# A hybrid decoder step on one core: where VectorE's evictions of the attention levels stand in the second mixer

## Chip, core and metric

The kernel runs on one NeuronCore of a Trainium2 chip. The metric is the device time of one launch in microseconds (us), the median of several runs. Engines are called TensorE (PE in the rows, PEld for its weight loads), VectorE (DVE), ScalarE (ACT), GpSimd (POOL) and SyncE (SP, which issues the DMAs). Each runs its own instructions strictly in their order and waits on semaphores.

## What is computed

Two decoder layers run over 512 new prompt tokens and 32 sample tokens (8 sequences of 4): a half-step SwiGLU feed-forward, a token mixer, a second feed-forward and a gated per-layer embedding. The first layer's mixer is GLA, the second's is HGRN2. Both rest on one recurrence with a decay per channel; within a block of tokens it is exact pairwise attention:

```python
def chunked_gated_linear_recurrence(q, k, v, g, s0, scale):
    # S_t = diag(exp(g_t)) S_{t-1} + k_t^T v_t ; o_t = scale * q_t S_t
    ...
        b = jnp.cumsum(gc, axis=1)
        rel = b[:, :, None] - b[:, None, :]
        decay = jnp.exp(jnp.where(mask, rel, -jnp.inf))
        attn = jnp.einsum('bthk,bshk,btshk->bhts', qc, kc, decay) * scale
        o_intra = jnp.einsum('bhts,bshv->bthv', attn, vc)
        o_inter = jnp.einsum('bthk,bhkv->bthv', qc * jnp.exp(b), S) * scale
        k_dec = kc * jnp.exp(b_last[:, None] - b)
        S_new = S * jnp.exp(b_last)[..., None] + jnp.einsum('bshk,bshv->bhkv', k_dec, vc)

def hgrn2_mixer(u, w_in, gn, w_out, lb, s0):
    q, f, i, g = jnp.split(u @ w_in, cuts, axis=-1)
    log_f = jnp.logaddexp(jnp.log(lb), jnp.log1p(-lb) + jax.nn.log_sigmoid(f))
    k = (1.0 - lb) * jax.nn.sigmoid(-f)
    o, s = chunked_gated_linear_recurrence(heads(jax.nn.silu(q)), heads(k), heads(i), heads(log_f), s0, 1.0)
    o = rms_norm(o, gn) * jax.nn.silu(heads(g))
    return o.reshape(B, T, HGRN_I_DIM) @ w_out, s
```

## The kernel before

Every matmul with weights is done three times, on a high and a low part of both operands, to keep float32 accuracy. Weights come in units of 512 KB through a ring of four slots; ScalarE copies the high part (`high`), VectorE subtracts it for the low part (`low`, the tile `w_low`). `ahead(n)` does this two units ahead of TensorE.

Each mixer is done in two head groups, numbered 0 and 1 (GLA, 2 heads each) and 2 and 3 (HGRN2, 4 heads each). The attention of a 128-token chunk is split by levels. Level l takes blocks of 2L tokens (L = 2 to the l, l from 0 to 6) and computes the second half's queries against the first half's keys; the decay across the half's border is put into the two factors. For each level:

- VectorE sums the gates up to the block (`level_gates`, L2043, tile `gate_sum`) and takes the differences to the border (`level_diffs`, L2031, tile `ex`), both in place for the level to come.
- ScalarE takes their exponentials (`level_keys` L1424 for the differences, `level_queries` L1408 for the sums).
- VectorE multiplies keys and queries with them (`level_keys` L2059, tile `k_tilde`; `level_queries` L2087, tile `q_tilde`). In the GLA groups GpSimd does the queries' part.
- TensorE computes eight blocks of 128 x 128 (L828) into PSUM banks 4 and 5 (banks 6 and 7 for level 5).
- VectorE (ScalarE for levels 5 and 6) copies the wanted parts under a mask into the tile `attn` (`level_out`, the *eviction*, L2010; for levels 0 and 1 also a small one for the sample tokens, L1999 and L2019).

In groups 2 and 3 levels 0 to 4 share banks 4 and 5, so TensorE's level l waits for the eviction of level l - 1 (semaphore `lvl_out`) besides the products of its own level (`kt_made`, `qt_made`). Between the levels TensorE computes other tiles of the same stage, by a table written out by hand (`gr.steps`): gate tile g0, four units of the value matmul (L773) with levels 0 to 3 behind them, gate tile g1 with levels 4 and 5 behind it, g2 with level 6, and at last g3. The value matmul fills banks 0 to 3 and 7. Gate tile g1 uses banks 0 and 1 and waits until ScalarE has evicted the first two value tiles (`values_out`, L1386, semaphore `v_out`); on ScalarE these evictions stand behind the two exponentials of level 4, the other three behind those of level 5.

Behind the levels (`mix`), VectorE evicts g2 (L1881), makes the keys' decays to the chunk's end (L2152, L2156), splits two weight units (L1677) and multiplies the decays into the keys (L2165, semaphore `kdec_made`). TensorE transposes these keys (L863) after g3. SyncE loads the sample states in two halves of four DMAs (L477): the first when all levels are computed, the second when the decays of all keys are in, since the destination overlaps tiles that are read until then. TensorE's products with those states (L902) wait for all of them (`s0_in`).

Of the kernel before, what the change touches and what calls it, by code (L numbers as in the profile page):

```python
# [154 lines left out]
def _build(nc, a, o, ctx):  # L155
# [128 lines left out]
    def halves(ap):  # L284
        return ap.rearrange("p (a b) -> p a b", a=2)
# [57 lines left out]
    def samples(t, gr):  # L343

        return t[:, gr.NH * T_PROMPT:gr.NH * T]
# [1326 lines left out]
    def _(dve):  # L1672
# [235 lines left out]
        def features(gr):  # L1908
            n = gr.start
            qs = [(Q, h, gr.q_scale if gr.gla else None) for h in range(gr.NH)]  # L1910
            ks = [(K, h, None) for h in range(gr.NH)]
            dests = ([(RT, None, None)] if gr.has_r else []) + (qs + ks if gr.gla else ks + qs)
            if gr.gi == 1:

                dve.wait_ge(s["x_out"], 4)
                dve.tensor_copy(halves(G[:, 0:2 * T_PROMPT]), OG[:, 6:8, 0:T_PROMPT])
                dve.tensor_copy(halves(samples(G, gr)), OG[:, 6:8, T_PROMPT:T]).then_inc(s["x_made"], 1)
                dve.wait_ge(s["x_made"], 1)
            for j, (dst, h, scale) in enumerate(dests):
                if not gr.gla and j == 5:  # L1920
                    log_sigmoid(gr)
                    gate(gr)
                    head_out(gr, j, n, dst, h, scale)
                    gate_diff(gr)
                    ahead(n)
                    gate_key(gr)
                    n += 1
                    continue
                if not gr.gla and j == 7:
                    gate_end(gr)  # L1930
                ahead(n)
                if gr.gi == 1 and j == 1:
                    log_sigmoid(gr)
                if gr.g == 1 and j == 0:
                    dve.wait_ge(s["og_made"], 2 * gr.gi)
                    dve.wait_ge(s["og_made_p"], 2 * gr.gi)
                if h is None:
                    feature_out(gr, j, n, dst)
                else:
                    head_out(gr, j, n, dst, h, scale)  # L1940
                n += 1
                if gr.g == 0 and j == 1:
                    sample_tokens(gr)
                if gr.g == 1 and j in (0, 2):
                    sequences(GROUPS[gr.gi - 1], j // 2)
                if gr.has_r and j >= gr.nfeat - 2:
                    gates_out(gr, range(2) if j == gr.nfeat - 2 else (2,))
            if gr.gi == 0:
                log_sigmoid(gr)
            for kind, j, levels in gr.steps[:-2]:  # L1950
                ahead(n)
                n += 1
                for lv in levels:
                    if lv == "diag":
                        if gr.gla:
                            level_gates(gr, 0)
                        feature_out(gr, gr.nfeat, n - 1, OG[:, 4 * gr.g, :])
                        if not gr.gla:
                            level_queries(gr, 0)
                            level_gates(gr, 0)  # L1960
                        if gr.has_r:
                            gates_out(gr, (3,))
                        diagonal(gr)
                        level_diffs(gr, 1)
                    elif lv and lv < 4:
                        level(gr, lv)
                        level_out(gr, lv - 1)
            level(gr, 4)
            level_out(gr, 3)
            level(gr, 5)  # L1970
            ahead(n)
            feature_out(gr, gr.nfeat + 1, n, OG[:, 4 * gr.g + 1, :])
            level_out(gr, 4)
            level_keys(gr, 6)
            if not gr.gla:
                level_queries(gr, 6)
            level_gates(gr, 6)
            if gr.gla:
                ahead(n + 1)
            else:  # L1980
                feature_out(gr, gr.nfeat + 2, gr.g3_unit - 1, OG[:, 4 * gr.g + 2, :])
# [9 lines left out]
        def level_out(gr, l):  # L1991
            gi, NH = gr.gi, gr.NH
            n, L = LEVELS * gi + l, 1 << l
            b0 = gr.level_bank(l)
            dve.wait_ge(s["lvl_mm"], n + 1)

            if l == 0:
                S = T_SAMPLE
                dve.tensor_tensor(ATS[0:S, 0:NH, :], ps[0:S, 6, 0:NH * 32].rearrange("p (x n) -> p x n", x=NH),  # L1999
                                  ident[0:S, 0:S].rearrange("p (o n) -> p o n", o=1).to_broadcast([S, NH, S]),  # L2000
                                  ALU.mult).then_inc(s["sdiag_out"], 1)
                dve.wait_ge(s["diag_out"], gi + 1)
                dve.wait_ge(s["sdiag_out"], gi + 1)
            else:
                dve.wait_ge(s["lvl_out"], n)
            if l == 1:
                dve.wait_ge(s["slvl_out"], 2 * gi + 1)
            msk = [(0, 2 * NH), (L, 64 // L), (1, L)]
            for r in range(2):
                ins = dve.copy_predicated(query_half(AT, gr, L, r), view(masks[:, l, r, :].bitcast(U32), 0, msk),  # L2010
                                          compact(psf[:, 512 * b0:512 * b0 + 1024], gr, L, r))
            ins.then_inc(s["lvl_out"], 1)
            if l < 2:
                S = T_SAMPLE
                dst = ATS[0:S, 0:NH, :].rearrange("p x (n l) -> p x n l", l=2 * L)[:, :, :, L:2 * L]
                data = ps[0:S, 6, (8 + 4 * l) * 16:(8 + 4 * l + NH) * 16].rearrange("p (x n l) -> p x n l", x=NH, l=L)
                msk = masks[0:S, l, 0, 0:S // 2].bitcast(U32).rearrange("p (o n l) -> p o n l", o=1, l=L)\
                    .to_broadcast([S, NH, 16 // L, L])
                dve.copy_predicated(dst, msk, data).then_inc(s["slvl_out"], 1)  # L2019

        def level_diffs(gr, l):

            gi, L = gr.gi, 1 << l
            dve.wait_ge(s["gate_made"], (LEVELS + 1) * gi + l + 1)
            if l > 1:
                dve.wait_ge(s["kt_made"], (LEVELS - 1) * gi + l - 1)
            if l == 1:
                g1, _, tot = sample_blocks(G, gr, L)
                dve.tensor_tensor(sample_compact(DK, gr, L), tot, g1, ALU.subtract)
            for r in range(2):  # L2030
                ins = dve.tensor_tensor(compact(DK, gr, L, r), last_key(G, gr, L, r), key_half(G, gr, L, r), ALU.subtract)  # L2031
            ins.then_inc(s["diff_made"], 1)

        def level_gates(gr, l):

            n, L = LEVELS * gr.gi + l, 1 << l
            dve.wait_ge(s["eq_made"], n + 1)
            if l < 2:
                _, g2, tot = sample_blocks(G, gr, L)
                dve.tensor_tensor(g2, g2, tot, ALU.add)  # L2040
            for r in range(2):
                g2 = query_half(G, gr, L, r)
                ins = dve.tensor_tensor(g2, g2, last_key(G, gr, L, r), ALU.add)  # L2043
            ins.then_inc(s["gate_made"], 1)
# [15 lines left out]
                                        compact(DK, gr, L, r), ALU.mult)  # L2060
            ins.then_inc(s["kt_made"], 1)

        def level(gr, l):

            level_keys(gr, l)
            if not gr.gla:
                level_queries(gr, l)
            level_gates(gr, l)
            level_diffs(gr, l + 1)

        def level_queries(gr, l):

            gi, L = gr.gi, 1 << l
            n = LEVELS * gi + l
            dve.wait_ge(s["eq_made"], n + 1)
            if l >= 2:
                dve.wait_ge(s["lvl_mm"], n - 1)
            if l == 0:
                if gr.g == 1:
                    dve.wait_ge(s["lvl_mm"], LEVELS * gi)  # L2080
                dve.wait_ge(s["feat_out"], gr.feat0 + gr.nfeat)
                dve.wait_ge(s["q_made"], 2 * (gi - 1))
            if l < 2:
                dve.tensor_tensor(QTS[:, l, 0:gr.NH * 16].rearrange("p (n l) -> p n l", l=L),
                                  sample_blocks(Q, gr, L)[1], sample_compact(EQ, gr, L), ALU.mult)
            for r in range(2):
                ins = dve.tensor_tensor(compact(QTb[:, l % 2, :], gr, L, r), query_half(Q, gr, L, r),  # L2087
                                        compact(EQ, gr, L, r), ALU.mult)
            ins.then_inc(s["qt_made"], 1)
# [417 lines left out]
```

## Time and profile before

| | |
|---|---|
| median of 3 runs | 2235.97 us (2233.2 to 2236.51) |
| the profiled execution | 2235.69 us, its span 2233.3 us |
| TensorE busy | 2213.9 us (99%), granted clock 0.997 on the mean |
| VectorE busy | 1577.2 us (71%) |
| ScalarE busy | 1083.9 us (49%) |
| GpSimd busy | 332.3 us (15%) |

The two head groups of the second mixer compute their levels from about 1517 to 1568 us and from about 1657 to 1708 us. In the rows a time at the head of a line is microseconds from the span's start, the next number how long the instructions of the line took together. An instruction gives way to the next on its engine a little ahead of its end, so a line may overlap the next. A bracket names the idle time of the engine just before and what ended it.

### The profile page before, as it was taken

What the parts mean: (1) busy time and instruction counts of PE and PEld (TensorE: products, weight loads), DVE (VectorE), ACT (ScalarE), POOL (GpSimd) and SP (SyncE); (2) the same over time, 40 slices, a digit from 0 to 9 for tenths busy, and PEclk for the clock granted to TensorE, in tenths of its full rate; (3) what the DMA queues carried; (4) which work ended last, traced back from release to release, by engine and by line L of the source; (5) the groups of instructions that cost most, each with busy time, mean ns of one, the idle gap of its engine ahead of it and who ended that gap; (6) DMA issues with size and microseconds to landing.
All of it is one profiled execution on the core that took longest, in us unless ns stands there. A gap on an engine that the chain in (4) does not pass through costs nothing. (4 is left out here: it accounts for less than half of the span.)

```text
span 2233.3 us, 42317 instructions
## 1 busy us (share of the span) xinstructions
PE 2213.9 (99%) x17778; PEld 2168.5 (97%) x17778; DVE 1577.2 (71%) x2172; ACT 1083.9 (49%) x1573; POOL 332.3 (15%) x239
## 2 busy tenths in 40 slices
PE   9999999999999999999999999999999999999998
PEld 8999999989999999999999999998999999999998
DVE  7888833567678888535788884359688788886344
ACT  7555622443555555423655562255465565555234
POOL 3222101112111221000222210000000212220001
PEclk9999999999999999999999999999999999999999
DMA  4333333233352333333233333322333333333231
GB/s 136 102 107 95 102 100 83 58 105 93 102 137 76 107 102 102 91 102 86 67 110 99 95 100 95 105 71 67 91 95 105 104 91 95 111 97 107 83 96 49
DMA packets 387338, 213.36 MB, mean 96 GB/s; under 512 B 7007, under 2 KB 381438, under 8 KB 387150
## 3 DMA queue, kind: packets, MB, share of 16 engines
q1 hardware_dynamic: 386928, 210.59, 33.6%
q8 instruction: 140, 2.29, 0.4%
q14 instruction: 48, 0.39, 0.1%
q10 hardware_dynamic: 190, 0.05, 0.0%
q0 software_dynamic: 32, 0.03, 0.0%
HBM read 198.98 MB, written 11.67 MB: 94 GB/s over the span
## 5 line engine op out<-in xcount | busy, mean ns | idle before, releaser
L642 PE MATMUL ps<-u_diffs,w_high 128*128 128x272 f32 x2560 | 486.8, 288 | 2.3 <-DVE w_low L1773 1.7
L642 PEld LDWEIGHTS ps<-u_diffs,w_high 128*128 128x128 f32 x2560 | 402.1, 188 | 3.2 <-issue 3.0
L642 PE MATMUL ps<-u_diffs,w_low 128*128 128x272 f32 x1280 | 369.3, 289 | 0.0
L1677 DVE TENSOR_TENSOR w_low<-w_raw,w_high 128x1024 fp32r<-128x1024 f32 x205 | 259.1, 1281 | 98.1 <-ACT w_high L1136 97.8
L2399 POOL TENSOR_TENSOR hidden<-t_gate,t_up 128x544 f32<-128x544 f32 x84 | 190.1, 2263 | 717.7 <-ACT t_gate L1258 717.7
L570 PE MATMUL ps<-hid_high,w_high 128*128 128x272 f32 x1408 | 290.4, 287 | 0.0
L570 PE MATMUL ps<-hid_high,w_low 128*128 128x272 f32 x1408 | 289.5, 288 | 0.0
L570 PE MATMUL ps<-hid_low,w_high 128*128 128x272 f32 x1408 | 289.1, 287 | 0.0
L642 PE MATMUL ps<-u_high,w_low 128*128 128x272 f32 x960 | 277.5, 289 | 0.0
L642 PE MATMUL ps<-u_low,w_high 128*128 128x272 f32 x960 | 276.9, 288 | 0.0
L642 PE MATMUL ps<-u_high,w_high 128*128 128x272 f32 x960 | 275.9, 287 | 0.3 <-DVE w_low L1773 0.3
L1136 ACT ACTIVATE w_high<-w_raw 128x1024 fp32r<-128x1024 f32 x205 | 210.4, 1049 | 113.4 <-PE ps L570 73.6
L570 PE MATMUL ps<-u_high,w_high 128*128 128x272 f32 (+2 forms) x1168 | 245.7, 292 | 2.2 <-DVE u_low L1690 1.8
L642 PEld LDWEIGHTS ps<-u_diffs,w_low 128*128 128x128 f32 x1280 | 240.6, 188 | 0.0
L570 PE MATMUL ps<-u_high,w_low 128*128 128x272 f32 (+2 forms) x1168 | 240.4, 288 | 0.0
L570 PE MATMUL ps<-u_low,w_high 128*128 128x272 f32 (+2 forms) x1168 | 240.3, 287 | 0.0
L1773 DVE TENSOR_TENSOR w_low<-w_sums,w_high 128x512 fp32r<-128x512 f32 (+1 forms) x240 | 208.6, 869 | 21.5 <-ACT w_high L1227 20.5
L570 PEld LDWEIGHTS ps<-hid_low,w_high 128*128 128x128 f32 x1408 | 220.1, 188 | 0.0
L570 PEld LDWEIGHTS ps<-hid_high,w_low 128*128 128x128 f32 x1408 | 219.3, 188 | 0.0
L570 PEld LDWEIGHTS ps<-hid_high,w_high 128*128 128x128 f32 x1408 | 219.2, 188 | 0.0
L1161 ACT ACTIVATE u_high<-h_resid,vectors 128x544 fp32r<-128x544 f32 x48 | 36.1, 751 | 372.7 <-DVE h_resid L1873 322.3
L570 PEld LDWEIGHTS ps<-u_high,w_high 128*128 128x128 f32 x1168 | 184.1, 188 | 5.6 <-DVE u_low L1690 2.4
(292 smaller groups left out, 4093.7 us busy)
## 6 DMA issues: line engine op xcount, KB each, us to landing
w_raw<-in_ffn_w_gu_dram SPq DMA_DIRECT2D x176, 512.0 KB, 5.2
w_raw<-in_ffn_w_down_dram SPq DMA_DIRECT2D x64, 512.0 KB, 4.5
w_raw<-in_hgrn_w_in_dram SPq DMA_DIRECT2D x32, 512.0 KB, 4.7
w_raw<-in_gla_w_in_dram SPq DMA_DIRECT2D x25, 512.0 KB, 5.0
w_raw<-in_ffn_w_down_dram SPq DMA_DIRECT2D x32, 384.0 KB, 4.5
w_raw<-in_ple_w_gate_dram SPq DMA_DIRECT2D x16, 512.0 KB, 4.9
states_s<-in_state_gla_dram SPq DMA_DIRECT2D x8, 512.0 KB, 5.9
out_gla_s_dram<-states_s SPq DMA_DIRECT2D x8, 512.0 KB, 3.8
```

The costliest lines, as they stand in the source:

```text
L570: mm = pe.matmul(ps[:, bank + hf, 0:t1 - t0], weights(slot, w0 + k, wk, m0, P, kw), x[:, kk - w0, t0:t1], start=(kk == 0 and part == 0), s ...
L642: mm = pe.matmul(ps[:, bank, 0:HALF], half_slot(w, base, h)[:, k * P:(k + 1) * P], x(k), start=start and k == 0 and part == 0, stop=k == K ...
L1136: act.activation(WH[:, slot, :], RAW[:, slot, :], ACT.Copy).then_inc(s["hi_made"], 1)
L1161: act.activation(flat_of(UH, m), flat_of(H, m), ACT.Copy, scale=gain_of(e, m)).then_inc(s["uh_done"], 1)
L1677: dve.tensor_tensor(WL[:, slot, :], RAW[:, slot, :], WH[:, slot, :].bitcast(F32), ALU.subtract)\
L1773: dve.tensor_tensor(half_slot(WL, base, h, n), src, half_slot(WH, base, h, n).bitcast(F32), ALU.subtract)\
L2399: pool.tensor_tensor(HID[:, f, :], tG[:, :], tU[:, :], ALU.mult).then_inc(s["hid_mul"], 1)
```

## The change

In the HGRN2 groups, the eviction of level l - 1 moves, for l from 1 to 4, from behind the gate sums of level l and the differences of level l + 1 to a place ahead of them, right behind the products of level l. The eviction of level 4 stays where it was, and so does everything in the GLA groups. TensorE's, ScalarE's, GpSimd's and SyncE's instructions and their order are the same.

```diff
@@ features
                     elif lv and lv < 4:
                         level(gr, lv)
-                        level_out(gr, lv - 1)
             level(gr, 4)
-            level_out(gr, 3)
-            level(gr, 5)
+            level(gr, 5, False)
@@ level
-        def level(gr, l):
+        def level(gr, l, out=True):
 
             level_keys(gr, l)
             if not gr.gla:
                 level_queries(gr, l)
+                if out:
+                    level_out(gr, l - 1)
             level_gates(gr, l)
             level_diffs(gr, l + 1)
+            if gr.gla and out:
+                level_out(gr, l - 1)
```

VectorE in group 2, level 1 and the start of level 2, before (`w_low` is a weight split, `ex` the differences, `attn` and `attn_s` the evictions):

```order
L2087 TENSOR_TENSOR q_tilde<-q,ex 128x8x64 x2
L2040 TENSOR_TENSOR gate_sum<-gate_sum 128x32x2
L2043 TENSOR_TENSOR gate_sum<-gate_sum 128x8x32x2 x2
L2031 TENSOR_TENSOR ex<-gate_sum 128x8x64 x2
L1999 TENSOR_TENSOR attn_s<-ps,ident 32x128
L2010 COPY_PREDICATED attn<-masks,ps 128x8x64 x2
L2019 COPY_PREDICATED attn_s<-masks,ps 32x64
L1677 TENSOR_TENSOR w_low<-w_raw,w_high 128x1024
L2059 TENSOR_TENSOR k_tilde<-k,ex 128x128x4 x2
```

The same place on VectorE after the change (the lines from L1964 on are two lower):

```order
L2089 TENSOR_TENSOR q_tilde<-q,ex 128x8x64 x2
L1997 TENSOR_TENSOR attn_s<-ps,ident 32x128
L2008 COPY_PREDICATED attn<-masks,ps 128x8x64 x2
L2017 COPY_PREDICATED attn_s<-masks,ps 32x64
L2038 TENSOR_TENSOR gate_sum<-gate_sum 128x32x2
L2041 TENSOR_TENSOR gate_sum<-gate_sum 128x8x32x2 x2
L2029 TENSOR_TENSOR ex<-gate_sum 128x8x64 x2
L1677 TENSOR_TENSOR w_low<-w_raw,w_high 128x1024
L2057 TENSOR_TENSOR k_tilde<-k,ex 128x128x4 x2
```

The three instructions of the eviction of level 0 have moved up past the three of the sums and differences; the weight split still stands between the differences and the key products.

VectorE in group 2, level 4 and the start of level 5, before:

```order
L2059 TENSOR_TENSOR k_tilde<-k,ex 128x32x16 x2
L2087 TENSOR_TENSOR q_tilde<-q,ex 128x8x64 x2
L2043 TENSOR_TENSOR gate_sum<-gate_sum 128x8x4x16 x2
L2031 TENSOR_TENSOR ex<-gate_sum 128x8x64 x2
L2010 COPY_PREDICATED attn<-masks,ps 128x8x8x8 x2
L2059 TENSOR_TENSOR k_tilde<-k,ex 128x16x32 x2
L2087 TENSOR_TENSOR q_tilde<-q,ex 128x8x64 x2
```

The same place on VectorE after the change:

```order
L2057 TENSOR_TENSOR k_tilde<-k,ex 128x32x16 x2
L2089 TENSOR_TENSOR q_tilde<-q,ex 128x8x64 x2
L2008 COPY_PREDICATED attn<-masks,ps 128x8x8x8 x2
L2041 TENSOR_TENSOR gate_sum<-gate_sum 128x8x4x16 x2
L2029 TENSOR_TENSOR ex<-gate_sum 128x8x64 x2
L2057 TENSOR_TENSOR k_tilde<-k,ex 128x16x32 x2
L2089 TENSOR_TENSOR q_tilde<-q,ex 128x8x64 x2
```

The eviction of level 3 has moved up past the sums and differences, and the key products of level 5 now follow the differences directly. The same holds one level earlier.

## Rows read from the trace of the kernel before

**Rows 1.** The page's first part: busy time of TensorE, share, instructions.

```profile
PE 2213.9 (99%) x17778; PEld 2168.5 (97%) x17778; DVE 1577.2 (71%) x2172; ACT 1083.9 (49%) x1573; POOL 332.3 (15%) x239
```

**Rows 2.** TensorE's waits over the span: us in total, times, longest.

```profile
PE ps L828 <- DVE attn L2010: 2.8, 4, 1.0
PE ps L1094 <- ACT y_feat L1147: 2.6, 1, 2.6
```

**Rows 3.** Timeline of TensorE: last value matmul, levels 1, 2; level 1 again, group 3.

```profile
1530.43 0.40 PE L773 MATMUL ps<-w_low,u_high 128*128 128x512 f32 x1
1531.84 0.57 PE L828 MATMUL ps<-q_tilde,k_tilde 128*128 128x128 f32 x3 [1.01 <-DVE attn L2010]
...
1540.36 0.91 PE L828 MATMUL ps<-q_tilde,k_tilde 128*128 128x128 f32 x6 [0.40 <-DVE attn L2010]
...
1671.49 0.68 PE L828 MATMUL ps<-q_tilde,k_tilde 128*128 128x128 f32 x4 [1.02 <-DVE attn L2010]
```

**Rows 4.** Timeline of VectorE, group 2, sums of level 1 to eviction of level 0.

```profile
1526.17 0.21 DVE L2040 TENSOR_TENSOR gate_sum<-gate_sum 128x64 f32<-128x64 f32 x1
...
1527.63 1.29 DVE L2031 TENSOR_TENSOR ex<-gate_sum 128x512 f32<-128x512 f32 x2
1528.84 0.27 DVE L1999 TENSOR_TENSOR attn_s<-ps,ident 32x128 f32<-32x128 f32 x1
1529.21 2.48 DVE L2010 COPY_PREDICATED attn<-masks,ps 128x512 f32<-128x512 uint32 x2
```

**Rows 5.** Timeline of VectorE, group 2, differences of level 4 on; query products of level 5.

```profile
1545.03 1.30 DVE L2031 TENSOR_TENSOR ex<-gate_sum 128x512 f32<-128x512 f32 x2
1546.24 1.33 DVE L2010 COPY_PREDICATED attn<-masks,ps 128x512 f32<-128x512 uint32 x2
1547.55 1.29 DVE L2059 TENSOR_TENSOR k_tilde<-k,ex 128x512 f32<-128x512 f32 x2
...
1555.02 1.28 DVE L2087 TENSOR_TENSOR q_tilde<-q,ex 128x512 f32<-128x512 f32 x2
```

**Rows 6.** Timeline of ScalarE, group 2, exponentials of level 4 and first value tiles.

```profile
1546.36 1.06 ACT L1424 ACTIVATE ex<-ex 128x1024 f32<-128x1024 f32 x1 [6.43 <-DVE ex L2031]
1547.33 1.14 ACT L1408 ACTIVATE ex<-gate_sum 128x512 f32<-128x512 f32 x2
1549.18 1.27 ACT L1386 ACTIVATE v_tok<-ps,rstd_tok 128x512 f32<-128x512 f32 x2 [0.72 <-PE ps L773]
```

**Rows 7.** Timeline of TensorE, group 2, level 3 and the start of level 4.

```profile
1548.98 1.95 PE L828 MATMUL ps<-q_tilde,k_tilde 128*128 128x128 f32 x16
...
1556.75 0.72 PE L828 MATMUL ps<-q_tilde,k_tilde 128*128 128x128 f32 x5
```

**Rows 8.** Timeline of VectorE, group 2, eviction of gate tile g2 and key decays.

```profile
1566.51 0.72 DVE L1881 TENSOR_TENSOR out_gate<-ps,rstd 128x544 f32<-128x544 f32 x1 [1.06 <-PE ps L570]
...
1571.83 2.49 DVE L2165 TENSOR_TENSOR k<-k,ex 128x1024 f32<-128x1024 f32 x2
```

**Rows 9.** Timeline of SP's queue, the last state load of groups 2 and 3.

```profile
1576.54 0.51 SPq L477 DMA_DIRECT2D states_s<-in_state_hgrn_dram  x1
...
1715.50 0.51 SPq L477 DMA_DIRECT2D states_s<-in_state_hgrn_dram  x1
```

**Rows 10.** DMA issues, these two loads: count, KB each, us to landing.

```profile
states_s<-in_state_hgrn_dram SPq DMA_DIRECT2D x1, 256.0 KB, 5.0
...
states_s<-in_state_hgrn_dram SPq DMA_DIRECT2D x1, 256.0 KB, 5.1
```

**Rows 11.** Timeline of TensorE, products with the sample states, groups 2 and 3.

```profile
1581.62 0.65 PE L902 MATMUL ps<-states_s,q 128*32 128x128 f32 x16 [0.27 <-issue]
...
1720.92 0.84 PE L902 MATMUL ps<-states_s,q 128*32 128x128 f32 x21
```

**Rows 12.** Stretches near the end: busy PE, PEld, DVE, ACT, POOL; granted clock; DMA.

```profile
2218.00:2220.00 2.00, 0.46 (x5) 0.22 (x2) 1.45 (x4) 0.83 (x2) 0.00 (x0) 1.00 0.00 0
...
2224.00:2226.00 2.00, 1.79 (x9) 1.69 (x10) 1.48 (x2) 1.57 (x5) 0.00 (x0) 0.50 0.00 0
```

## Prediction, on record before the run

> **What bounds the kernel now.** I read the engines' shares first, then who TensorE waited for, then the timelines of TensorE, VectorE and ScalarE through the second mixer, then the DMA queue. TensorE is busy 2213.9 of 2233.3 us [rows 1]: a change can only take away what little it idles, or add idle time. Its largest wait in total is for the block evictions on VectorE, four times, 2.8 us [rows 2]. All four lie in the second mixer: before levels 1 and 2, in head group 2 (near 1531 and 1540 us) and again in head group 3 (near 1671 and 1680) [rows 3]. The view counts from a matmul's modelled end. Counted from the step of the value matmuls (0.23 us, from one start to the next), TensorE could have gone on at 1530.43 + 0.23 = 1530.66 and went on at 1531.84: 1.18 us lost. The view gives 1.01 of that; its 0.40 at level 2 is 0.56 counted so. The first matmuls after each wait cost some 0.07 more. **So the stalls that the change aims at are worth 1.25 + 0.63 = 1.9 us per head group, 3.8 us in all, 0.17% of the run.** A measurement of this kernel can tell about 0.2% (4.5 us) from no change; even the whole gain is below that. Group 3 runs the same pattern 139.65 us later, so I work out group 2 and carry it over.
>
> **Part 1, the evictions come earlier (gain 1.9 us per group at first).** VectorE's slot after the query products of level 1 opens at 1526.17. Before, it holds the gate sums; the differences follow at 1527.63, the eviction of level 0 at 1529.21, 2.48 long, and TensorE starts 0.15 after its end [rows 3, 4]. After, the sample eviction takes this slot (it takes 0.37 up to the main one, by 1528.84 and 1529.21), the main one runs from 1526.54 to 1529.02, and TensorE, free at 1530.66, does not wait. The same holds at level 2: TensorE gets there 1540.36 - 0.56 - 1.25 = 1538.55; the eviction of level 1, which ended 0.15 ahead of 1540.36, moves up by the 2.53 of a level's sums and differences (from 1526.17 to 1528.84, less 0.14 for the small sum at its head) less the 0.14 of part 2, and ends at 1537.8. Level 3 had no wait and has none.
>
> **Part 2, what the eviction had covered is open now (VectorE 2.74 us late).** From the differences' start of level l+1, ScalarE's exponential starts 1.33 us later (1545.03 to 1546.36), and the key products that need it 1.19 after that (1546.36 to 1547.55): 2.52 in all. The differences fill 1.21 of it, up to 1546.24 [rows 5, 6]. Before, the eviction of the level below stood in the other 1.31, up to 1547.55. Its own share is some 1.23 (it lasts 1.33, less the 0.1 by which such instructions overlap: the differences last 1.30 and give way after 1.21); 0.08 was waiting even then. After, it takes its 1.23 ahead of the sums, and where nothing else stands in the gap, the 1.31 pass empty: 1.23 lost. At levels 2 and 3 a weight split of some 1.18 us still stands there (1.23 long), so only about 0.14 is lost each time. At levels 4 and 5 nothing does. VectorE's lateness against the old times: 0.14 at level 2's keys, 0.28 at level 3's, 1.51 at level 4's, 2.74 at level 5's (2 x 0.14 + 2 x 1.23). The gap ahead of level 6 is covered by a weight split, the gate eviction and the eviction of level 4, in both kernels, and stays at 2.74.
>
> **Part 3, where TensorE meets this (the 1.9 us are gone at the next gate tile).** Behind level 3 TensorE computes gate tile g1 in PSUM banks 0 and 1. It must wait until ScalarE has evicted the first two value tiles from them, and ScalarE does that only behind the two exponentials of level 4. Before: exponentials at 1546.36 and 1547.33, values from 1549.18, 1.27 long, done at 1550.45; TensorE begins g1 at about 1550.9, behind the sixteen matmuls that it starts at 1548.98 (16 in 1.95 us), unhindered [rows 6, 7]. The exponentials hang on the differences of level 4, which are now 1.51 late, so they start at 1547.9 and 1548.9, the values at 1549.9, done at 1551.2, and g1 starts at 1551.3. TensorE would be there at 1550.86 - 1.9 = 1548.96. **It waits about 2.4 us, and g1 begins 0.45 later than before.** After g1, level 4 begins at 1557.2 instead of 1556.75. Level 5 needs the query products that end 2.74 late, at 1559.05: TensorE, there at 1559.15, starts at 1559.25, 0.6 late. Level 6 and the transposes behind it follow 0.8 to 0.9 late by the same addition.
>
> **Part 4, the state loads (what sets the end of each group).** Before, VectorE has 1.06 us of idle time ahead of the eviction of gate tile g2; that takes up part of the 2.74, and TensorE's g2 itself ends about 0.8 late, so the eviction and all behind it are 2.74 - 1.14 = 1.6 late (the idle time plus the 0.08 by which an instruction gives way ahead of its end), the decays of the keys at 1571.83 among them [rows 8]. The second half of the sample-state loads waits in SP's queue for just these decays. Its last load, issued at 1576.54, takes 5.0 us to land: 1581.54 [rows 9, 10]. TensorE starts the products with these states at 1581.62 after 0.27 us of idle time that the view calls issue [rows 11]: 0.08 after the landing, so I take it that this load already ended the wait. With the load 1.6 late, group 2 is 1.6 us late. In group 3 the load lands at 1715.50 + 5.1 = 1720.60 and TensorE comes at 1720.92, 0.24 us of slack after the same 0.08: 1.6 - 0.24 = 1.36, more than the 0.9 by TensorE's own way.
>
> **What lies under cover.** The weight splits late by up to 2.74 are for g3 and for the next stage's units; g3 is needed 5 us or more after its split. The next loads of weights go behind the state loads in SP's queue, for tiles used over 15 us later. GpSimd has no part in these levels. The first mixer keeps its order.
>
> **Sum.** 1.6 + 1.36 is 2.96. The profiled execution took 2235.69 us (2.4 more than its span, unchanged by this) and stands 0.3 below the median of the three runs: 2235.69 + 2.96 = 2238.65, and I predict 2238.7.
>
> **A rule against the trace, twice.** The last state load takes 5.0 and 5.1 us [rows 10]. The Trainium skill, "DMA: Bandwidth & Descriptors" (Anatomy of one DMA, SWDGE path), gives a transfer about 2 us plus its bytes at 436 GB/s; by an estimate from that page 256 KB alone would take 2.6 us, and by it the loads would be hidden. The rows here disagree, for four loads issued 0.5 us apart behind one another. The second rule is at rival 3.
>
> **Rivals.**
> 1. Gain only, 2235.69 - 3.8 = 2231.9: if g1 did not wait for ScalarE (the semaphore of the value tiles is in the code, but the trace of before shows no wait there). Against it: ScalarE's queue order is fixed, and slack was just 0.4 us.
> 2. The loads are hidden and TensorE's own way decides: 0.9 per group, 2237.5. For it: landings can vary, and 0.7 us less would do.
> 3. The clock falls. At the end of the program TensorE waits 2.6 us for ScalarE [rows 2], its busy time falls to 0.46 of 2 us, and the granted clock goes from 1.00 to 0.50, from 2.4 to 1.2 GHz [rows 12], some microseconds later. The new wait before g1 is 2.4 us long. If it does the same, half the rate over g1's 5.9 us costs up to 5.9 per group, over half of it 3: 2238.65 + 6 to 12, taken as 2244.7. It decides only where the clock falls in both or one of the groups. Against it: in the tail few and tiny matmuls followed the wait; here dense ones stand on both sides. The Trainium skill, "TensorE: Matmul & The Clock Gate" (Part 1: The HAM clock gate), says too that an idle array is put back to half rate; the tail agrees, no row shows it for a wait between dense matmuls.
> 4. The loads land later than before (they then share the DMA engines with weight loads at another place): 0.8 us more in each group gives 2240.3, beyond that the run is slower by over 0.2%.
> That the change doesn't do what it says is no rival: the order of VectorE shows it.
>
> **Chances.** Forecast 0.59; rival 1 0.07; rival 2 0.12; rival 3 0.14; rival 4 beyond 0.8 us 0.08. Faster by over 0.2% would need rival 1 and a low run: 0.02. Slower by over 0.2%: rivals 3 and 4 and a little of the noise, 0.22. Within 0.2%: 0.76. The range leaves out rival 1 and the far part of rival 3: from 2235.5 (rival 2 less the 2 us by which runs of one kernel differ) to 2243.5. The forecast's own range is 2237.3 to 2240.
>
> **What would show it.** Right: no wait for the evictions before levels 1 and 2; a wait of about 2.4 us before g1 for ScalarE's value tiles, with the granted clock at 1.00; VectorE idle for some 1.2 us ahead of the key products of levels 4 and 5; the key decays 1.6 us later against the query products of level 1, and a longer wait before the state products. Wrong: g1 without a wait (Part 3), key products of level 5 as early as before (Part 2), the state loads landing well ahead of TensorE (Part 4).

## The result and the profile after

The changed kernel took 2243.11 us (median of 6 runs, 2241.42 to 2243.94), the kernel before 2235.57 us beside it (6 runs, 2232.96 to 2236.51): a ratio of 1.0031, 95% interval 1.0020 to 1.0042. It is 7.5 us slower, by more than the 0.2% that can be told from no change. On another occasion, with 27 runs of the kernel before beside it, it was 2242.09 against 2236.22 (ratio 1.0029, 1.0018 to 1.0040). The forecast was 2238.7; the time lies in the range and near the 2244.7 of rival 3.

The profiled execution after took 2243.67 us, 7.98 more than the one before; its span is 8.5 longer. The first lines of its page, against [rows 1]:

```profile
span 2241.8 us, 42317 instructions
PE 2222.1 (99%) x17778; PEld 2177.3 (97%) x17778; DVE 1577.0 (70%) x2172; ACT 1083.9 (48%) x1573; POOL 333.3 (15%) x239
```

The same instructions are there, and VectorE and ScalarE are as busy as before. TensorE is busy 8.2 us longer with the same 17778 matmuls. So all but 0.3 us of the loss is busy time: **the matmuls themselves ran slower somewhere.** TensorE's waits (us in total, times, longest), against [rows 2]:

```profile
PE ps L570 <- ACT v_tok L1386: 4.6, 2, 2.4
PE ps L1094 <- ACT y_feat L1147: 2.6, 1, 2.6
PE ps L902 <- issue: 0.2, 1, 0.2
```

The four waits for the evictions, 2.8 us, are gone. In their place stand two for the value tiles on ScalarE, ahead of gate tile g1, one in each head group, 4.6 us. The timeline of TensorE through group 2, against [rows 3] and [rows 7] (start, length together, idle time before in the bracket):

```profile
1531.45 0.39 PE L773 MATMUL ps<-w_low,u_high 128*128 128x512 f32 x1
1531.68 0.38 PE L828 MATMUL ps<-q_tilde,k_tilde 128*128 128x128 f32 x2
...
1539.57 0.83 PE L828 MATMUL ps<-q_tilde,k_tilde 128*128 128x128 f32 x6
...
1548.11 1.95 PE L828 MATMUL ps<-q_tilde,k_tilde 128*128 128x128 f32 x16
1552.19 0.82 PE L570 MATMUL ps<-u_high,w_high 128*128 128x272 f32 x2 [2.13 <-ACT v_tok L1386]
1552.81 0.66 PE L570 MATMUL ps<-u_low,w_high 128*128 128x272 f32 x2
...
1559.80 3.73 PE L828 MATMUL ps<-q_tilde,k_tilde 128*128 128x128 f32 x32
```

Levels 1 to 3 (1531.68, 1539.57, 1548.11) follow their predecessors without a gap. Then comes the wait, and behind it two matmuls of 272 columns take 0.66 us, which took 0.41 before. VectorE in the same stretch, against [rows 5] and [rows 8]:

```profile
1547.56 1.29 DVE L2029 TENSOR_TENSOR ex<-gate_sum 128x512 f32<-128x512 f32 x2
1550.08 1.29 DVE L2057 TENSOR_TENSOR k_tilde<-k,ex 128x512 f32<-128x512 f32 x2 [1.22 <-PE ps L828]
...
1555.01 1.30 DVE L2029 TENSOR_TENSOR ex<-gate_sum 128x512 f32<-128x512 f32 x2
1557.53 1.29 DVE L2057 TENSOR_TENSOR k_tilde<-k,ex 128x512 f32<-128x512 f32 x2 [1.22 <-ACT ex L1424]
...
1569.56 0.72 DVE L1881 TENSOR_TENSOR out_gate<-ps,rstd 128x544 f32<-128x544 f32 x1 [0.37 <-PE ps L570]
```

VectorE idles 1.22 us between the differences and the key products of levels 4 and 5. (The first bracket names TensorE, which had long been done with what the key products need of it; the exponential ends 0.13 us ahead of this start.) ScalarE, against [rows 6]:

```profile
1548.89 1.06 ACT L1424 ACTIVATE ex<-ex 128x1024 f32<-128x1024 f32 x1 [5.35 <-DVE ex L2029]
1549.85 1.13 ACT L1408 ACTIVATE ex<-gate_sum 128x512 f32<-128x512 f32 x2
1550.89 1.24 ACT L1386 ACTIVATE v_tok<-ps,rstd_tok 128x512 f32<-128x512 f32 x2
```

The exponentials wait for the differences, the value tiles stand behind the exponentials, and g1 starts 0.06 us after their end at 1552.13. Last, stretches of the kernel after (busy time of PE, PEld, DVE, ACT, POOL; granted clock; DMA), the first two around the wait in group 2, the third in group 3, the others behind the state products of groups 2 and 3:

```profile
1549.80:1552.20 2.40, 0.27 (x4) 0.07 (x2) 2.12 (x4) 2.34 (x5) 0.00 (x0) 0.99 0.75 182
1552.20:1555.60 3.40, 3.40 (x15) 3.40 (x16) 3.37 (x6) 0.00 (x0) 0.00 (x0) 0.50 0.00 0
...
1695.60:1698.90 3.30, 3.15 (x14) 3.15 (x15) 3.27 (x6) 0.10 (x1) 0.00 (x0) 0.50 0.00 0
...
1593.20:1596.50 3.30, 3.30 (x17) 3.30 (x17) 1.04 (x2) 0.98 (x3) 0.00 (x0) 0.50 0.00 0
1736.50:1739.90 3.40, 3.40 (x17) 3.40 (x17) 1.09 (x2) 1.35 (x3) 0.00 (x0) 0.50 0.00 0
```

The same stretches of the kernel before (over g1, and behind the state products of group 2), and one at the end of the first mixer:

```profile
1550.80:1554.20 3.40, 3.40 (x30) 3.40 (x29) 3.37 (x6) 1.58 (x3) 0.00 (x0) 1.00 0.50 122
1590.40:1593.70 3.30, 3.30 (x20) 2.34 (x20) 2.11 (x4) 2.65 (x4) 0.00 (x0) 1.00 0.00 0
...
598.70:602.10 3.40, 3.40 (x16) 3.03 (x15) 1.84 (x4) 1.94 (x4) 0.00 (x0) 0.50 0.00 0
```

**As soon as the wait ends, TensorE runs at half its clock, 1.2 of 2.4 GHz, over the first 3.4 us of g1**: 15 matmul instructions where the kernel before does 30 in the same time. The Trainium skill, "TensorE: Matmul & The Clock Gate" (Part 1: The HAM clock gate), says that an idle array is put back to half rate; here the trace agrees.

The falls at the groups' ends are of another kind. TensorE idles 0.33 us at most there; ahead of the fall at 1593.13 it does small products:

```profile
1590.48 1.07 PE L933 MATMUL ps<-attn_s,v_tok 32*128 32x32 f32 x8
1591.48 2.15 PE L938 MATMUL ps<-sample_rows,gate_sum 128*128 128x32 f32 x16
```

The stretch at 0.50 near 598.70 in the kernel before follows the same two groups of products at the end of the first mixer, from 595.43 on.

The next table compares how far each kernel is, counted from the first matmul of level 0 in its own group, with the first profile of the kernel before (from TensorE's timelines; there g1 starts at 1550.68 - 1521.64 = 29.04, by the lines below). "Keys turned" is the transpose ahead of the last state work (L917), "head sums" the last matmul (L954) of the heads' mean squares behind it.

| us later than before, groups 2 / 3 | g1 | level 4 | state products | keys turned | head sums |
|---|---|---|---|---|---|
| after | 0.5 / 0.8 | 2.0 / 2.3 | 2.0 / 2.3 | 2.0 / 2.3 | 3.6 / 3.9 |
| after, second profile | 0.5 / 0.9 | 2.1 / 2.4 | 2.7 / 2.4 | 2.7 / 2.4 | 2.7 / 4.1 |
| before, second profile | 0.0 / 0.0 | 0.0 / 0.0 | -0.3 / 0.6 | -0.3 / 0.6 | -0.3 / 0.6 |
| before, third profile | 0.0 / 0.0 | 0.0 / 0.0 | -0.2 / 0.0 | -0.2 / 0.0 | 1.4 / 1.6 |

```profile
1521.64 1.95 PE L828 MATMUL ps<-q_tilde,k_tilde 128*128 128x128 f32 x16
...
1550.68 0.50 PE L570 MATMUL ps<-u_high,w_high 128*128 128x272 f32 x2
```

So the 8.5 us between the two spans are: 2.0 and 2.3 in the groups up to the turned keys, of which the clock over g1 gives 1.5 each (level 4 less g1); 1.6 and 1.6 from falls of the clock at the groups' ends; and 1.0 ahead of group 2, where a fall at the end of the first mixer's first group, near 494 us, meets a start that went 0.6 better. Of this only the lateness up to level 4 (2.0 and 2.3, 2.1 and 2.4) stands in both profiles of the changed kernel; the other falls come in some executions and not in others, as the runs below show.

### The profile page after: what moved, and what is told of

The parts are those of the page before. It is cut to its first block and busy times, and to the rows that moved or that the text cites. A ratio compares the mean times of both kernels' runs of the same rounds, so it can differ in the third digit from the quotient of the medians.

```text
span 2241.8 us, 42317 instructions
## 1 busy us (share of the span) xinstructions
PE 2222.1 (99%) x17778; PEld 2177.3 (97%) x17778; DVE 1577.0 (70%) x2172; ACT 1083.9 (48%) x1573; POOL 333.3 (15%) x239
```

## The experiments

All were run beside the kernel before; the ratio is to its runs of the same occasion. Where nothing else is said, a diff is against the changed kernel. In the texts put down ahead of each run, theory A is that the wait and the fall of the clock behind it are the loss.

**The changed kernel again.**

> The changed kernel again, for a second profile. If the two falls of the clock at the ends of the second mixer's groups (near 1593 and 1736 us of the first profile) and the one in the first mixer are a matter of the single execution, they stand elsewhere or are missing here, while those over g1 stand in both. If they follow from the change, all stand at the same places. Time as measured, 7.5 us above the kernel before.

2242.09 us (6 runs), ratio 1.0029 (1.0018 to 1.0040). The wait before g1 is there in both groups, 4.6 us, and the low clock over g1 in both (near 1552 and 1695). At the groups' ends only group 3 has a fall. In the first mixer the falls near 494 and 600 us stand again, and both also stand in the second profile of the kernel before. Two stretches of this kernel:

```profile
1552.10:1555.40 3.30, 3.30 (x15) 3.30 (x16) 3.27 (x6) 0.00 (x0) 0.00 (x0) 0.50 0.00 0
...
1592.00:1595.50 3.50, 3.50 (x32) 3.50 (x32) 0.96 (x3) 0.97 (x3) 0.00 (x0) 1.00 0.00 0
```

**Only the evictions of levels 0 and 1 early.**

```diff
-                if out:
+                if out and l in (1, 2):
                     level_out(gr, l - 1)
             level_gates(gr, l)
             level_diffs(gr, l + 1)
-            if gr.gla and out:
+            if out and (gr.gla or l not in (1, 2)):
                 level_out(gr, l - 1)
```

> Only the evictions of levels 0 and 1 stand ahead of the sums; those of levels 2 and 3 stay behind the differences as before. Theory A (the loss is the wait that the early evictions of levels 2 and 3 make before gate tile g1, and the fall of TensorE's clock that this wait sets off): the differences of level 4 are only 0.3 us late, no wait over 1.2 us anywhere in the levels, a new one of about 0.95 before level 3 for the eviction of level 2, granted clock 1.00 at g1, each group 0.7 us shorter: 1.4 us below the kernel before (ratio 0.9994). Rival B (the order itself costs VectorE time, whatever the level): about half the loss of the changed kernel, 3 to 4 us above the kernel before.

2236.07 us (11 runs), ratio 0.9997 (0.9989 to 1.0006): no loss, and a gain too small to be told. In the profile g1 is 0.7 and 0.35 us earlier than before and the keys are turned 0.34 earlier in both groups, half of what theory A said. TensorE waits before level 3, now for the eviction of level 2 (0.75 us in group 2, 1.10 in group 3), and g1 follows without a wait, at a granted clock of 1.00:

```profile
1546.78 2.02 PE L828 MATMUL ps<-q_tilde,k_tilde 128*128 128x128 f32 x16 [0.75 <-DVE attn L2008]
1548.76 0.52 PE L570 MATMUL ps<-u_high,w_high 128*128 128x272 f32 x2
```

```profile
1548.00:1552.00 4.00, 4.00 (x34) 3.86 (x33) 3.96 (x7) 1.00 (x3) 0.00 (x0) 1.00 0.33 80
```

The order itself costs nothing where something fills the gap behind the differences. Rival B, half the loss, is out.

**Only the evictions of levels 2 and 3 early** (the same edit with 3, 4 in place of 1, 2).

> Only the evictions of levels 2 and 3 stand ahead of the sums; levels 0 and 1 keep the old order and their two waits. VectorE is late by the same 2.46 us at level 5, but TensorE has saved nothing ahead of g1. Theory A: the wait before g1 is 0.2 us, the clock stays at 1.00 there, the lateness reaches TensorE through level 6 and the state loads only, 1.3 and 1.1 us: 2.4 us above the kernel before (ratio 1.0011). Rival B (VectorE's lateness is the cost, by late products and late state loads, the clock a side effect): 6 to 7.5 us above, as in the changed kernel.

2238.92 us (12 runs), ratio 1.0015 (1.0007 to 1.0024), 2.7 us above where theory A said 2.4; Rival B, 6 us or more, is out. g1 starts 0.2 late with no wait, and no low clock stands near it:

```profile
1548.75 1.95 PE L828 MATMUL ps<-q_tilde,k_tilde 128*128 128x128 f32 x16
1550.63 0.52 PE L570 MATMUL ps<-u_high,w_high 128*128 128x272 f32 x2
```

Levels 5 and 6 are 0.3 and 0.5 late, and the keys are turned 0.5 and 0.9 late: 1.4 us in the two groups, where theory A had 2.4. That the median comes near 2.4 is in part chance; the profile has one more fall at a group's end. By the turned keys, VectorE's lateness by itself, with the old start of the levels, costs 1.4 of the changed kernel's 4.3 us. The medians of the two halves apart are -0.2 and +2.7; together they give 6 to 7.5. What the first half gains, the second makes into a wait.

**The wait filled with work, too much.**

```diff
             elif j == gr.nfeat + 1:
+                if not gr.gla:
+                    pe.wait_ge(s["slvl_out"], 2 * gr.gi + 2)
+                    for i in range(19):
+                        pe.matmul(ps[:, 6, 3 * P:4 * P], ones[:, :], ones[:, :], start=True, stop=True)
                 pe.wait_ge(s["v_out"], 5 * gr.gi + 2)
```

> The changed kernel with 19 matmuls of 128 columns more before gate tile g1 in groups 2 and 3 (about 2.2 us, ones by ones, into a free part of PSUM bank 6 that nobody reads), so that TensorE works through the wait. Theory A: the granted clock stays at 1.00 over g1, g1 takes 5.9 us instead of 7.4, the low levels of VectorE decide as in the prediction, 3.0 us above the kernel before instead of 7.5 (some 1.5 us less per fall that stays away, and the falls at the mixers' ends still to come or not). Rival B (lateness alone): as the changed kernel, 7.5 us above. Rival C (TensorE's work is what counts): 2 x 2.2 us above the changed kernel.

2241.69 us (8 runs), ratio 1.0023 (1.0014 to 1.0033). A float32 matmul is two instructions here, so the 19 took some 4.2 us, not 2.2, and g1 started 2.4 late in both groups, 1.9 in group 2 past the start that the wait allowed. No low clock stands over g1: it took its old time, and level 4 was 2.4 late too. It shows that the clock stays up if TensorE works; the size, 5.5 us above where theory A said 3.0, says nothing.

**The wait filled with work, to measure** (10 in place of 19).

> As e3_fill with 10 matmuls instead of 19: those took 0.224 us each there, 4.25 in all, and pushed g1 1.9 us past the end of the wait; ten take 2.2 us and end with it. Theory A (the wait before g1 costs its fall of the clock): no wait over 0.4 us before g1, the granted clock 1.00 over g1, g1 0.5 us later than in the kernel before (counted from level 0's first matmul), level 4 also 0.5 instead of 2.0 to 2.4, and only then the late state loads decide, 1.6 and 1.36 us at the state products: 3.0 us above the kernel before, some 3 us below the changed one. Rival B (late VectorE work costs the same with or without the fall): as the changed kernel, 6 to 7.5 above.

2240.19 us (11 runs), ratio 1.0013 (1.0004 to 1.0022). g1 starts 0.5 and 0.8 late, as in the changed kernel, but level 4 follows 0.5 and 0.9 late, not 2.0 and 2.3. The keys are turned 0.9 and 2.0 late (predicted 1.6 and 1.4). The stretch over g1's start in group 2, level 4 there (level 0 starts at 1521.29), and the first matmuls of g1 in group 3 with the filling ahead of them:

```profile
1549.00:1552.00 3.00, 3.00 (x27) 2.91 (x26) 3.00 (x6) 1.77 (x4) 0.00 (x0) 1.00 0.41 100
```

```profile
1556.91 1.28 PE L832 MATMUL ps<-q_tilde,k_tilde 128*128 128x128 f32 x10
...
1690.65 2.40 PE L721 MATMUL ps<-ones 128*128 128x128 f32 x20
1693.30 0.52 PE L570 MATMUL ps<-u_high,w_high 128*128 128x272 f32 x2 [0.25 <-ACT v_tok L1390]
```

With TensorE's own useful work unchanged and 20 filling instructions in the place of each wait, the median is 3.4 above the kernel before, against 7.5 and 5.9 of the changed kernel. That is near theory A's forecast (3.0), and what the prediction's sum without the clock said (2.96). The intervals of the ratios (up to 1.0022 here, from 1.0018 and 1.0020 there) overlap a little, so the times alone don't settle it; the profiles do. The time of g1's start is the same in both kernels, and 1.5 us per group at level 4 are the clock, not VectorE.

**The wait alone**, in the kernel before:

```diff
             level_queries(gr, 4)
+            if not gr.gla:
+                act.wait_ge(s["mm_units"], gr.v_unit + 4)
+                act.wait_ge(s["vs_mm"], 2 * gr.gi + 2)
+                act.activation(EP[:, :], Q[:, :], ACT.Copy)
+                act.activation(tG[:, :], Q[:, 0:T], ACT.Copy)
             values_out(gr, (0, 1))
```

> The kernel before, with its old order, and two more copies on ScalarE (2.0 and 0.6 us, from the queries into tiles that are free there) ahead of the eviction of the first two value tiles in groups 2 and 3: the wait before g1 alone, 2.3 us, while VectorE is late by 0.3 us at most. Theory A: the clock falls over g1 in both groups, level 4 starts 3.8 us later counted from level 0, and each group is 3.8 us longer: 7.7 above the kernel before. If the fall needs more than the wait: 2.3 us per group, 4.6 above, clock 1.00 over g1.

2244.62 us (6 runs), ratio 1.0030 (1.0017 to 1.0042), 7.8 above; theory A said 7.7. (The copy into `tG` overwrites the sample tokens that group 3 reads later, so the sample results of that group are others; the work is the same.) VectorE keeps its old order and idles only 0.15 us ahead of level 5's key products in group 2. g1 starts 2.3 late in both groups, level 4 3.8 late, and it stays 3.5 and 3.9 to the end. Both groups run more than 3 us of g1 at half the clock. The first line holds the wait, from 1550.67 to 1552.69, and the first 0.9 us of g1:

```profile
1550.00:1553.60 3.60, 1.58 (x13) 1.39 (x13) 3.52 (x6) 3.60 (x6) 0.00 (x0) 1.00 0.68 165
1553.70:1556.90 3.20, 3.20 (x16) 3.20 (x15) 3.19 (x6) 3.14 (x8) 0.00 (x0) 0.50 0.00 0
1697.00:1700.30 3.30, 3.30 (x16) 3.30 (x16) 3.30 (x6) 3.24 (x8) 0.00 (x0) 0.50 0.02 5
```

The interval of the ratio, 3.8 to 9.4 us, would hold the 4.6 of a wait without a fall too; the clock in the rows decides. With VectorE in its old order the wait alone makes the clock fall, and the fall costs 1.6 us on top of the 2.3.

**Three evictions early, that of level 3 in its old place.**

> Evictions of levels 0, 1 and 2 ahead of the sums, that of level 3 in its old place. The differences of level 4 are as late as in the changed kernel (1.5 us), so the wait before g1 is the same 2.3 us and the clock falls; VectorE is 1.2 us less late from level 5 on. Theory A: each group 2.0 us longer as in the changed kernel, 6 to 7 us above the kernel before. Rival B (VectorE's lateness at the end of the levels and the state loads decide): 0.5 us per group, 1 us above.

2242.29 us (11 runs), ratio 1.0022 (1.0014 to 1.0031), 5.5 above. The wait before g1 is the same (4.6 us in the two groups). In this profile the clock stayed up behind it in group 2 and fell in group 3:

```profile
1550.30:1555.00 4.70, 4.09 (x32) 4.09 (x33) 4.67 (x8) 1.69 (x3) 0.00 (x0) 1.00 0.02 7
1693.20:1696.50 3.30, 3.30 (x17) 3.30 (x16) 3.27 (x6) 0.80 (x1) 0.00 (x0) 0.50 0.02 5
```

Level 4 is 0.5 late in group 2 and 2.4 in group 3, the turned keys 0.2 and 2.4: one kernel, the same wait, with and without the fall. So a fall behind such a wait is likely, not certain, and where it stays away the group loses 0.2 us. Rival B, 1 us, lies below the interval (3.1 to 6.9 us). Beside the run with levels 0 and 1 alone, which has no wait before g1, it also shows that moving level 2's eviction is what adds the wait.

**The value tiles first on ScalarE.**

```diff
+            if not gr.gla:
+                values_out(gr, (0, 1))
             level_keys(gr, 4)
             level_queries(gr, 4)
-            values_out(gr, (0, 1))
+            if gr.gla:
+                values_out(gr, (0, 1))
```

> The changed kernel with ScalarE's eviction of the first two value tiles ahead of the two exponentials of level 4 in groups 2 and 3. The wait before g1 goes, and the exponentials come 0.7 us later still. Theory A: VectorE's chain is the cause of the wait, so it turns up again at level 5, for the key and query products, 3.0 us long, and the clock falls behind it: each group 2.2 us longer plus up to 1.5 for the fall, 5 to 7.5 us above the kernel before. If the place on ScalarE was the cause: the gain of 1.9 us per group is kept, 2 to 4 us below the kernel before.

2241.26 us (11 runs), ratio 1.0024 (1.0015 to 1.0033), 4.5 above, a little less than theory A's 5 to 7.5 and far from a gain. The gain of 1.9 us is kept through g1 and level 4, in both groups; then TensorE waits 2.9 us for the query products of level 5, and the clock falls there:

```profile
1554.43 1.95 PE L828 MATMUL ps<-q_tilde,k_tilde 128*128 128x128 f32 x16
1559.25 3.65 PE L828 MATMUL ps<-q_tilde,k_tilde 128*128 128x128 f32 x16 [2.88 <-DVE q_tilde L2092]
```

The same sixteen matmuls take 1.95 us ahead of the wait and 3.65 behind it. In group 3 the same wait ends at 1701.40 and the fall comes at 1702.68, 1.3 us later. The place on ScalarE only chooses where the wait stands; VectorE's chain makes it.

**The kernel before, twice more.**

> The kernel before again, for another profile. If the falls of the clock at the ends of the second mixer's groups (behind the state products, some 70 us after level 0's first matmul) are a matter of the single execution, they can stand here too, and its time is then 1.4 us above the first profile's for each. If they come from the change alone, there is none. The stretch over g1 is at 1.00 in either case.

> The same once more, since one profile may have none by chance: at least one fall at a mixer's end in the two profiles if they are a matter of the single execution (six of the profiles of the other kernels have one or two).

2236.56 and 2239.68 us, one run each. The second of the two has a fall at each group's end:

```profile
1591.00:1594.00 3.00, 3.00 (x9) 1.97 (x9) 2.17 (x3) 2.18 (x3) 0.00 (x0) 0.50 0.00 0
1732.00:1736.00 4.00, 4.00 (x16) 2.96 (x15) 2.27 (x3) 2.82 (x4) 0.00 (x0) 0.75 0.00 0
```

So these falls are a matter of the single execution and come in the kernel before too; its first profile just had none. Of the nine profiles of the other kernels, seven have one or two of them (the text above says six), among them the kernel with only levels 0 and 1 early, which has no wait before g1. Three profiles of the kernel before are too few to say whether it has them less often.

## Why the prediction was right, and where it was not

The time lies within the stated range, 0.4 us below its upper end of 2243.5, and outside the forecast's own range of 2237.3 to 2240. Parts 1 to 3 came as worked out; that the range held is owed to the share of rival 3 in it, and in part to luck.

**Part 1, right.** Level 1 starts 1.17 us earlier (1.18 worked out), level 2 1.81 and level 3 1.89 (1.9), in both groups. Every wait for an eviction is gone.

**Part 2, right.** VectorE idles 1.22 us ahead of the key products of levels 4 and 5 (1.23). Those of level 5 start at 1557.53, 3.72 after the time of before; group 2 began 1.0 late in that execution (level 0 at 1522.66), so 2.7 are its own (2.74).

**Part 3, right, with one reading 0.2 us off.** TensorE waits 2.1 and 2.4 us before g1 by the view, 2.4 and 2.7 counted from the step of the matmuls as the prediction counts (2.4); g1 starts 0.5 and 0.8 late (0.45). The start of g1 that the sum uses, 1550.86, is 1550.68 in the record; with it the same sum gives a wait of 2.5 and a lateness of 0.6. With the wait filled, level 5 is 0.6 late in group 2 (0.6). The 0.3 more in group 3 come from VectorE: it idles 0.44 us ahead of level 2's key products there, 0.08 in group 2, and the differences of level 4 are 1.8 late instead of 1.5; what it waits for stays open.

**Part 4, right in kind, decided by something else.** The decays hung on VectorE as said, and without the fall the loads decide: with the wait filled, the keys are turned 0.9 and 2.0 late, 2.8 together, where the sum had 2.96. But the split between the groups was not met. In group 2 the decays come 1.56 late (1.6), yet the last load goes out only 0.9 late, since one of the four issues takes SyncE 0.51 us instead of 1.20. The landings vary by themselves too: the kernel before moves its state products by -0.3 and +0.6 us between two profiles. In the changed kernel TensorE comes 2.0 us later anyway, by the fall, and waits only 0.2 for the loads. The 2.6 us that the prediction holds against the 5.0 of a load is no fair comparison: the Trainium skill, "DMA: Bandwidth & Descriptors" (Anatomy of one DMA, SWDGE path), gives that rule for transfers on GpSimd's path. SyncE issues these loads, four behind one another, so the rows here neither bear the rule out nor refute it.

**The step that failed is the weight on the clock.** The sum of 2.96 is that of the kernel without a fall, and the sign "with the granted clock at 1.00" was not met; what came is rival 3, which had 0.14. I argued that in the tail few and tiny matmuls followed the wait, whereas dense ones stand on both sides here. That was wrong: dense matmuls behind the wait do not keep the clock up. In the profiles with a fall behind such a wait it comes between 0.2 us before the end of the wait and 1.3 us after it. And the prediction reads the clock only in the tail [rows 12]. The trace of before has a stretch at 0.50 in its middle, near 598.70, shown above; the page's row of the clock, in slices of 56 us, prints nines there. It would have said that the clock can fall in the middle of the program, behind a few microseconds of small products.

**Rival 3's price was met for another reason.** I took 3 us for each group on top of the sum. A fall costs 1.5 to 1.6 (1.54 and 1.46 in the profile after, 1.56 and 1.58 with the wait alone), and part of that covers the late state loads, so only 0.4 and 0.9 come on top of 1.6 and 1.36. 2235.69 + 4.3 would be 2240. The other 1.6 to 3.2 us of the medians' difference are for the most part clock too, by the runs' own records: the time lost to the clock, (1 - granted clock) x span, is 12.9 us on the mean of the changed kernel's 12 runs and 7.7 on that of the 27 runs before, 5.2 more, where two falls of 3.4 us at half the clock are 3.4. The rest is worth about one more fall in each execution elsewhere. Such falls stand in both kernels; whether the change makes them more frequent or the samples differ stays open.

**The chances.** 0.22 for slower by over 0.2% was too low; 0.02 for faster was right. The range held the time because it reached to part of rival 3.

## What to carry to other kernels

- On an engine that runs in order, an instruction that seems to delay a partner may be the one that hides a round trip: between VectorE's differences and its own use of ScalarE's exponential lie 2.52 us, and the eviction was the filling. Before it is moved, look at what stands in that gap afterwards. Moving it only where a weight split still filled the gap cost nothing.
- Price a new wait of TensorE like these, of 2.0 to 2.9 us, with the clock behind it, not with its length alone: with the wait alone 2.3 us became 3.8. Ask for the granted clock in stretches of a few microseconds, in the kernel before too; a row of broad slices hides falls of 3.4 us.
- Matmuls that nobody needs, in the place of an unavoidable wait, kept the clock up in all four cases. They saved time (3.4 us above instead of 6 to 7.5) only when they ended with the wait; too many gave back what they saved.

## What the runs showed of the hardware beyond what I expected

- The fall behind a wait of 2.0 to 2.9 us between dense matmuls: seen in 9 of 10 such waits in the profiles (after 2 of 2, again 2 of 2, the wait alone 2 of 2, the values first 2 of 2, three levels 1 of 2), and never at the waits of up to 1.1 us before levels 1 to 3. One and the same length, 2.13 us, had a fall behind it in group 2 of the changed kernel and none in group 2 of the kernel with three evictions early.
- Falls without a wait of that length, near the end of a mixer's group, behind products with 32 columns, in some executions and not in others of the same kernel: in the three profiles of the kernel before, none, none and two in the second mixer. Those three spans are 2233.3, 2234.8 and 2237.9 us, at mean granted clocks of 0.997, 0.996 and 0.995, so such falls are likely a good part of why its runs lie between 2233 and 2240 us.
- A float32 matmul of 128 by 128 shows as two instructions of TensorE (20 for the ten that fill the wait), 0.12 us from one to the next.
